# Forgetting attention with stationary values for two heads side by side, its weights scaled by VectorE, and the recurrence's head norm on VectorE

## The reference

```python
def rms_norm_f32(x, g):
    return xf * lax.rsqrt(jnp.mean(xf * xf, axis=-1, keepdims=True) + EPS) * g

# hgrn2, behind the scan over chunks; o: (B, S, 4 heads, 128)
    o = rms_norm_f32(o, norm_g)
    gate = jax.nn.silu(g).reshape(B, S, HGRN_HEADS, HGRN_DIM)
    return (o * gate).reshape(B, S, HALF)

def forgetting_attention(q, k, v, f_logit, b_f):
    c = jnp.cumsum(jax.nn.log_sigmoid(f_logit + b_f), axis=1).transpose(0, 2, 1)
    for blk in range(S // Q_BLOCK):                       # 4 query tiles of 128
        q0, q1 = blk * Q_BLOCK, (blk + 1) * Q_BLOCK
        logits = jnp.einsum('bqhd,bkhd->bhqk', q[:, q0:q1], k[:, :q1]) * scale
        logits = logits + c[:, :, q0:q1, None] - c[:, :, None, :q1]
        logits = jnp.where(kpos <= qpos, logits, -jnp.inf)
        p = jax.nn.softmax(logits, axis=-1)
        outs.append(jnp.einsum('bhqk,bkhd->bqhd', p, v[:, :q1]))

# the layer
    ya = hgrn2(...); yb = forgetting_attention(...)
    mix = jnp.concatenate([ya, yb], axis=-1) @ ev_w_out[e]
```

## Time and profile before

| | us |
|---|---|
| median of 3 runs | 2923.24 (2921.44 to 2928.81) |
| the profiled execution | 2928.32 |
| its span, first to last instruction | 2926.4 |
| PE busy | 2849.7 (97%) |
| DVE busy | 1678.2 (57%) |
| ACT busy | 1073.3 (37%) |
| POOL busy | 993.9 (34%) |
| first scores of the forgetting attention | at 1889.0 |
| first output product behind it | at 1941.70 |

### The profile page before, as it was taken

The page is one execution under the profiler, slowest core; times in us unless marked ns, Lnnn a source line. Parts: engine busy times, 40 slices in busy tenths (PEclk is TensorE's granted clock), DMA queues, the critical chain, the costliest instruction groups (busy, mean ns, idle before and its releaser), DMA issues.

```text
span 2926.4 us, 42935 instructions
## 1 busy us (share of the span) xinstructions
PE 2849.7 (97%) x17688; PEld 2509.3 (86%) x17688; DVE 1678.2 (57%) x2092; ACT 1073.3 (37%) x1792; POOL 993.9 (34%) x795
## 2 busy tenths in 40 slices
PE   8989999999999999999999999999999998999998
PEld 7877888999888768889998887789998886699987
DVE  3844513988335495048882334738884247598832
ACT  2235313544124373235441221545442233454411
POOL 5840261000647612610016467530006464000063
PEclk9998999999999999999999999999999998999999
DMA  4341341433223203314322332004332232043322
GB/s 143 102 137 37 102 143 44 140 99 95 91 97 109 86 16 113 132 44 137 102 80 101 98 102 96 16 15 138 113 97 87 87 108 72 23 140 106 95 87 87
DMA packets 185862, 271.69 MB, mean 93 GB/s; under 512 B 7988, under 2 KB 147252, under 8 KB 185668
## 3 DMA queue, kind: packets, MB, share of 16 engines
q1 hardware_dynamic: 175520, 243.29, 25.6%
q10 hardware_dynamic: 10148, 25.66, 2.6%
HBM read 266.79 MB, written 2.13 MB: 92 GB/s over the span
## 4 chain that ended last, share of the span: by engine, by line
PE 81%; DVE 11%; issue 3%; DMA 2%; ACT 2%; POOL 1%; ACTq 0%; SPq 0%; DVEq 0%; POOLq 0%
PE PS L498 24%; PE PS L500 24%; PE PS L499 24%; PE PS L949 3%; PE PS L589 2%; DVE a_qk L1666 2%; PE PS L911 1%; POOL wlo L2781 1%; DVE nmx L2001 1%; PE PS L1105 1%; DVE s_c L2651 1%; PE PS L1852 1%; DVE rawb_r L1264 1%; DVE d_a L1995 0%; DMA rawb<-ffn_w 0%
## 5 line engine op out<-in xcount | busy, mean ns | idle before, releaser
L2781 POOL TENSOR_TENSOR wlo<-raw,whi 128x512 fp32r<-128x512 f32 x502 | 680.7, 1386 | 602.8 <-ACT whi L668 602.8
L2773 POOL TENSOR_SCALAR whi<-raw 128x1024 fp32r<-128x1024 f32 x224 | 258.9, 1175 | 1189.6 <-PE PS L500 814.3
L498 PE MATMUL PS<-xT_hi,ring_r 128*128 128x256 f32 x1280 | 362.5, 283 | 1.3 <-issue 1.3
L499 PE MATMUL PS<-xT_lo,ring_r 128*128 128x256 f32 x1280 | 362.2, 283 | 0.0
L498 PE MATMUL PS<-xT_hi,whi 128*128 128x512 f32 (+1 forms) x1024 | 349.0, 341 | 10.9 <-DVE xT_lo L609 6.4
L499 PE MATMUL PS<-xT_lo,whi 128*128 128x512 f32 (+1 forms) x1024 | 345.2, 337 | 0.0
L500 PE MATMUL PS<-xT_hi,wlo 128*128 128x512 f32 (+1 forms) x1024 | 345.1, 337 | 0.0
L498 PE MATMUL PS<-sum_hi_r,ring_r 128*128 128x256 f32 x960 | 272.5, 284 | 5.1 <-DVE u_u L1362 5.1
L498 PE MATMUL PS<-whi,hs_hi 128*128 128x512 f32 x704 | 274.7, 390 | 1.0 <-issue 1.0
L500 PE MATMUL PS<-whi,hs_lo 128*128 128x512 f32 x704 | 274.0, 389 | 0.0
L499 PE MATMUL PS<-wlo,hs_hi 128*128 128x512 f32 x704 | 274.0, 389 | 0.0
(11 more groups left out here) (438 smaller groups left out, 6026.7 us busy)
## 6 DMA issues: line engine op xcount, KB each, us to landing
rawb<-ffn_w_gu SPq DMA_DIRECT2D x60, 512.0 KB, 3.6
rawb<-ffn_w SPq DMA_DIRECT2D x60, 512.0 KB, 3.6
raw<-ffn_w SPq DMA_DIRECT2D x26, 1024.0 KB, 4.9
raw<-ffn_w_down SPq DMA_DIRECT2D x22, 1024.0 KB, 4.9
raw<-mem_wkv SPq DMA_DIRECT2D x16, 1024.0 KB, 5.4
raw<-even_w_in SPq DMA_DIRECT2D x14, 1024.0 KB, 5.1
raw<-ev_w_in SPq DMA_DIRECT2D x14, 1024.0 KB, 5.2
raw<-odd_w_in SPq DMA_DIRECT2D x12, 1024.0 KB, 5.1
```

The source lines that it names most:

```text
L498: pe.matmul(o, lhs[0], rhs[0], start=start, stop=False, skip_group_check=True)
L499: pe.matmul(o, lhs[0], rhs[1], start=False, stop=False, skip_group_check=True)
L2773: pool.tensor_scalar(whi[b][:, cs], raw[b][:, cs], 1.0, 1.0, ALU.mult, ALU.mult).then_inc(panel_hi, 1)
L2781: m = pool.tensor_tensor(wlo[b][:, cs], raw[b][:, cs], whi[b][:, cs].bitcast(F32), ALU.subtract)
```

## The change

- The forgetting attention becomes `direct`: values stand still (64 columns, one head in each half of the columns), transposed weights of 128 columns stream, the output comes transposed and goes from PSUM into `xT_hi` and `xT_lo` (`act_direct`, `dve_direct`). `store` no longer scales, and `g_row`'s last 512 columns are not used.
- The softmax weights are scaled instead: `scale(u)` on DVE makes one reciprocal for two units and scales their `f_p` in place, behind the statistics of the odd units, two units back. PE's transposes wait for the new semaphore `f_scaled`.
- `f_p` has 6 buffers, `lag` is 4, `behind` is 7. The buffers move into the area of dead tiles, and `f_c1` moves so that it is not overwritten.
- The head norm's three products for each tile go from POOL to DVE (`norm(t)`), behind units 13, 15, 17 and 19. The power stays on POOL.
- At the end PE transposes only the recurrence's half of each tile (4 blocks).

```diff
@@ -257,10 +258,10 @@
         g_khr = w("g_khr", [P, S])
         g_qh = w("g_qh", [P, S])
         g_state = w("g_state", [P, NT, P])
-        f_c1 = w("f_c1", [P, 4, S])
-        w = Area("X")
+        w = Area("W")
+        f_p = w("f_p", [P, 6, 512])
         f_add = w("f_add", [P, 2, 512])
-        f_p = w("f_p", [P, 3, 512])
+        w = Area("W", 4 * (4 + 4 + 4) * S)
         f_pt = w("f_pt", [P, 2, 512])
 
         w = Area("W")
...
@@ -989,9 +988,9 @@
         def softmax_exp(act, A, u, src, scale, width, p):
 
             act.wait_ge(stat_ready, A.u0 + u + 1)
-            if u >= 3:
-
-                act.wait_ge(pt_psum, A.u0 + u - 2)
+            if u >= A.ps_:
+
+                act.wait_ge(pt_psum, A.u0 + u - A.ps_ + 1)
             act.activation(p[:, 0:width], src, ACT.Exp, bias=nmx[:, u:u + 1], scale=scale,
                            accum_out=rsum[:, u:u + 1]).then_inc(exp_done, 1)
...
@@ -2066,11 +2065,12 @@
 
         def stage_hgrn(st, jobs):
             A = Units(8 * NT, lambda u: u // 8 + 1, [0, 1, 2, 3], [4, 5], [6, 7], lambda u: u // 8, stat_ready,
-                      lambda u: f_p[:, u % 3, :], lambda u: f_pt[:, u % 2, :], lambda u: u % 8 == 7)
-            A.together = 2
+                      lambda u: f_p[:, u % 6, :], lambda u: f_pt[:, u % 2, :], lambda u: u % 8 == 7, direct=True)
+            A.together, A.lag, A.ps_, A.behind = 2, 4, 6, 7
             names = ["f_cut", "f_sum", "f_read", "f_abs", "f_ln", "f_bc", "f_bc_read",
                      "lb_in", "lb_exp", "lb_done", "g_lf", "g_scan", "g_din", "g_exp", "g_ops", "g_sc", "g_msk", "g_cpy",
-                     "g_inter", "g_kht", "g_khc", "g_kv", "g_st", "g_store", "gq_in", "gq_done", "gs_in", "g_rms", "g_norm"]
+                     "g_inter", "g_kht", "g_khc", "g_kv", "g_st", "g_store", "gq_in", "gq_done", "gs_in", "g_rms", "g_norm",
+                     "f_scaled"]
             G = {n: S_(n) for n in names}
             chunk = lambda c: slice(128 * c, 128 * c + 128)
             NL = 8
...
@@ -2230,9 +2230,13 @@
 
                     if 1 <= u <= NT:
                         act.activation(g_b[:, u - 1, :], g_row[:, u - 1, 0:512], ACT.Square).then_inc(G["gq_done"], 1)
+                    if u % 8 == 1 and u > 8:
+                        act_direct(act, 4, A.ob(u - 2), A.group(u - 2), A.u0 + u - 1)
                 act_units(act, A, lambda u: softmax_exp(act, A, u, f_add[:, u % 2, 0:128 * A.nk(u)], -1.0,
                                                         128 * A.nk(u), A.p(u)), squares)
-                act_rows(act, 0, KD)
+                act_direct(act, 4, A.ob(A.n - 1), NT - 1, A.u0 + A.n)
+                for t in range(NT):
+                    act_turn(act, xT_hi, 0, 4, 2 * t, t)
 
             def dve(dve, step):
                 dve.wait_ge(*loads["levels"])
...
@@ -2376,9 +2380,31 @@
                         dve.wait_ge(G["gq_done"], t + 1)
                         step(dve.tensor_reduce(scol[:, 16 + 4 * t:20 + 4 * t],
                                                g_b[:, t, :].rearrange("p (h d) -> p h d", h=4), AX_X, ALU.add))
+                    if u in (13, 15, 17, 19):
+                        norm((u - 13) // 2)
                     if u == 6 + NT:
                         dve.tensor_scalar(scol[:, 16:32], scol[:, 16:32], 1.0 / 128, EPS, ALU.mult, ALU.add)\
                             .then_inc(G["gs_in"], 1)
+
+                def scale(u):
+
+                    dve.wait_ge(exp_done, A.u0 + u + 2)
+                    step(dve.reciprocal(rec[:, u:u + 2], rsum[:, u:u + 2]))
+                    for v in (u, u + 1):
+                        p = A.p(v)[:, 0:128 * A.nk(v)]
+                        dve.tensor_scalar(p, p, rec[:, v:v + 1], None, ALU.mult).then_inc(G["f_scaled"], 1)
+
+                def norm(t):
+
+                    if t == 0:
+                        dve.wait_ge(G["g_rms"], 1)
+                    v = g_row[:, t, 0:512].rearrange("p (h d) -> p h d", h=4)
+                    for n, factor in enumerate((scol[:, 4 * t:4 * t + 4].unsqueeze(2).to_broadcast([P, 4, 128]),
+                                                pcol("norm_g").unsqueeze(1).to_broadcast([P, 4, 128]),
+                                                g_g[:, t, :].rearrange("p (h d) -> p h d", h=4))):
+                        if n:
+                            dve.wait_ge(G["g_norm"], 3 * t + n)
+                        dve.tensor_tensor(v, v, factor, ALU.mult).then_inc(G["g_norm"], 1)
 
                 def stat(u):
                     t, h = u // 8, u % 8
...
@@ -2390,15 +2416,17 @@
                     dve.tensor_tensor_reduce(out=f_add[:, u % 2, 0:n], in0=PS[:, A.ps(u), 0:n], in1=f_c(h)[:, 0:n],
                                              scale=-1.0, scalar=-NEG, op0=ALU.add, op1=ALU.min,
                                              accum_out=nmx[:, u:u + 1]).then_inc(stat_ready, 1)
+                    if u % 2 == 1 and u >= 3:
+                        scale(u - 3)
+                    if u == A.n - 1:
+                        scale(u - 1)
                     norms(u)
 
                 def store(g, bank):
-                    step(dve.reciprocal(rec[:, 8 * g:8 * g + 8], rsum[:, 8 * g:8 * g + 8]))
-                    return dve.tensor_tensor(g_row[:, g, 512:1024].rearrange("p (h d) -> p h d", h=8),
-                                             PS[:, bank, :].rearrange("p (h d) -> p h d", h=8),
-                                             rec[:, 8 * g:8 * g + 8].unsqueeze(2).to_broadcast([P, 8, 64]), ALU.mult)
+                    dve_direct(dve, 4, bank, g)
                 dve_units(dve, A, stat, store)
-                dve_rows(dve, 0, KD)
+                for t in range(NT):
+                    dve_turn(dve, xT_hi, xT_lo, 0, 4, 2 * t, t)
 
             def pool(pool):
...
@@ -2411,16 +2439,6 @@
 
                 pool.wait_ge(G["gs_in"], 1)
                 pool.tensor_tensor(scol[:, 0:16], scol[:, 16:32], rec[:, 32:48], ALU.pow).then_inc(G["g_rms"], 1)
-                pool.wait_ge(G["g_rms"], 1)
-                n = 0
-                for t in range(NT):
-                    v = g_row[:, t, 0:512].rearrange("p (h d) -> p h d", h=4)
-                    for factor in (scol[:, 4 * t:4 * t + 4].unsqueeze(2).to_broadcast([P, 4, 128]),
-                                   pcol("norm_g").unsqueeze(1).to_broadcast([P, 4, 128]),
-                                   g_g[:, t, :].rearrange("p (h d) -> p h d", h=4)):
-                        pool.tensor_tensor(v, v, factor, ALU.mult).then_inc(G["g_norm"], 1)
-                        n += 1
-                        pool.wait_ge(G["g_norm"], n)
 
             def pe(pe):
                 pe_split(pe, jobs, 1)
...
@@ -2513,10 +2531,16 @@
 
                 def values(u, k):
                     h = u % 8
-                    return f_v[:, k, 64 * h:64 * h + 64], 64 * h, 64
-                pe_units(pe, A, scores, values, lambda u: (exp_done, A.u0 + u + 1))
+                    return f_v[:, k, 64 * h:64 * h + 64], slice(64 * (h % 2), 64 * (h % 2) + 64), 128 * (h // 2)
+                pe_units(pe, A, scores, values, lambda u: (G["f_scaled"], u + 1))
+                n_turn["pe"] += NT
                 pe.wait_ge(G["g_norm"], 3 * NT)
-                pe_rows(pe, g_row, KD, lambda t: A.g0 + t + 1)
+                before = n_turn["pe"]
+                for t in range(NT):
+                    if t == 3:
+
+                        pe.wait_ge(lo_ready, before - 1)
+                    pe_turn(pe, g_row[:, t, 0:512], 4, 2 * t)
             return {"act_load": act_load, "act": act, "dve": dve, "pe": pe, "pool": pool}
 
         def stage_lru(st, jobs):```

The norm on DVE comes to stand between the scaling of units 10 and 11 and the statistics of unit 14. DVE's list before, from behind the statistics of unit 10 to those of unit 12 (`f_add` and `nmx` are the statistics of one unit); from there to unit 18 it holds statistics alone:

```order
L2380 TENSOR_SCALAR scol<-scol 128x16
L2390 ISA f_add,nmx<-PS,f_c_211 128x256
L2390 ISA nmx 128x1
L2396 RECIPROCAL rec<-rsum 128x8
L2397 TENSOR_TENSOR g_row<-PS,rec 128x512
L2390 ISA f_add,nmx<-PS,f_c_224 128x256
L2390 ISA nmx 128x1
```

7 lines of the change are left out of this document (3 added, 4 removed).

## The result

The changed kernel took 2929.16 us (median of 18 runs, 2924.67 to 2943.06), the kernel before 2924.72 us in the same session (18 runs, 2919.76 to 2933.42). The ratio is 1.0021, 95% interval 1.0012 to 1.0030: slower by 0.2% (the two medians alone are 1.0015 apart, which the interval holds). The forecast was 2929.0 us and +0.20%. The profiled execution has a span of 2926.6 us. The total is right; the terms that make it up are partly wrong and partly cancel, as the traces show, so that the closeness of the sum is luck.

What follows compares the result with a forecast made beforehand. PE sets the pace, busy 97% of the span. Terms -4.4 - 1.5 + 1.0 + 1.1 + 5.6 + 4.0 = +5.8 us gave 2929.0 us by the median (+0.20%), range 2918.5 to 2936.

Steps and rivals of the forecast that it cites:

- value products: Forgetting attention on PE: pairs of units get shorter, as in the lru stage's form; -4.4 us.
- tail: Attention's end: sixteen output-row transposes fewer, but the first output product waits for a chain; 3.6 to 2.1, -1.5 us.
- drain: Attention's last pairs: PE idles for copies held up by the two transposed-weight buffers; +1.0 us.
- squares, units 6 to 9: DVE also sums squares there, so PE waits for the scaling of units 6 and 8; +1.1 us.
- norm's place and collision: DVE's norm ahead of statistics and scaling makes PE wait, +5.6 us; POOL's split lengthens DVE's instructions, +4.0 us.
- over 5 us: Unit 12 of the attention: PE's wait for weights would grow from 1.6 to over 5 us.
- its last part: List of signs: PE waits for scaled weights at units 12, 14, 16 and 18, the first over 4 us.
- The clock falls: Rival: PE's idle time in the attention drops its clock for some 20 us; +5 us more, 2934.0 us; chance 0.27.
- No collision: Rival: POOL's split meets mostly statistics or its panel is held up; +1.8, 2925.0 us; chance 0.17.
- The norm hides too: Rival: PE's head start and six weight buffers cover DVE's norm; -3.8, 2919.4 us; chance 0.15.
- The heads do not overlap: Rival: two heads' value products run one behind the other, 4.4 us not gained; +10.2, 2933.4 us; chance 0.04.
- price for DVE's scalings: Attention on DVE: a plain pair costs 1.5 to 2.3 us against PE's 2.5 to 3.7, so hidden.

Runs made afterwards that it cites:

- e10: e6, but POOL's panel split is held until DVE has scaled the last pair of weights; 2918.47 us, ratio 0.9988 to the kernel before.
- e2: The changed kernel, but POOL waits for the end of DVE's head norm before it splits its panel; 2927.25 us, ratio 1.0020 to the kernel before.
- e11: The changed kernel with only POOL's panel split held until the last scaling; 2926.10 us, ratio 1.0021 to the kernel before.
- e3: The changed kernel with four buffers for the transposed weights instead of two; 2927.48 us, ratio 1.0019 to the kernel before.
- e6: The changed kernel with POOL's split ahead of the attention, four transposed buffers, norm products spread singly over units 14 to 30; 2924.23 us, ratio 1.0003.
- e4: The kernel before with only the head norm moved from POOL to DVE, old value products kept; 2928.81 us, ratio 1.0020.
- e7: e6 with the two heads' value products one behind the other instead of alternating; 2926.28 us, ratio 1.0019 to the kernel before.
- e9: e6, but POOL's panel split waits until DVE has laid its last mask of the recurrence; 2918.77 us, ratio 0.9986 to the kernel before.
- e1: The changed kernel with the head norm's twelve products back on POOL; 2924.44 us, ratio 1.0008 to the kernel before.
- e8: The changed kernel with the norm back on POOL, POOL's split ahead of the attention, four transposed buffers; 2927.89 us, ratio 1.0011.
- e5: The changed kernel with POOL's panel split moved ahead of the attention, before the wait for the norm's input; 2930.79 us, ratio 1.0023.

## Why the prediction was right, and where it was not

The direction and the mechanism held: PE waits for DVE, which norms and scales beside POOL's split. The sum held by luck: +5.8 us forecast; +6.4 by the path, +6.1 by the ratio. Term by term, with what the traces show for the changed kernel:

| term | forecast | measured | from |
|---|---|---|---|
| value products | -4.4 | -3.45 | PE's time up to the last value product, idle out: 48.77 before, 45.32 in e10 |
| tail | -1.5 | -1.45 | 3.70 to 2.25 |
| drain | +1.0 | +1.74 | 0.38 + 0.34 + 0.24 + 0.78 at the end |
| squares, units 6 to 9 | +1.1 | 0 | no wait for a scaling there |
| norm's place and collision | +5.6, +4.0 | +4.7 | waits 3.66 + 0.50 + 0.54 |
| short waits for a buffer | none | about +2.5 | an estimate, below |
| low clock | rival | about +2.2 | 4.89 against 2.66 |

The measured column sums to about +6.3. The stage grew by 6.75, and the kernel before had 0.23 us of idle time of its own, so 0.7 us have no term. The norm, the collision and the squares were forecast 6.0 us too high; what the forecast lacked or had too low adds up to 6.5 us.

**Right.** The value products of two heads side by side and the tail, by rows of another stage with the same form. From four-block scores to the sixteen value records PE takes 2.14 us (1928.31 to 1930.45), in the lru stage 2.13 (2510.55 to 2512.68), and the records take 1.09 in both. (1924.56 to 1928.31 is 3.75 us, close to the 3.74 of the four-block pair in the forecast, but it is another thing: it holds only twelve value records and one short stop. Without the stop it is 3.53 us in e10.) The step "splits the waiting weight panel at once: ... exactly while DVE norms tile 0 and scales" is what the trace shows, and the prices of the earlier trace rows (1.45, 1.60) are those of the collision here (1.41 to 1.64). e2 and e11 take the split away from the norm with nothing else changed, and the long wait and the low clock go both times.

**Wrong: the size of the norm's term.** It rests on DVE's turn being longer than PE's. DVE's was within the forecast of 3.7 to 4.3 us: in e11 the waits for scalings are 3.74, 3.80 and 3.86 us apart. But "PE has in that time ... 2.5 us with two blocks, 3.1 with three" was too small. With the 0.62, 0.69 and 0.54 us of these waits taken off, PE's own turn is 3.1 us, and 3.3 with three blocks. The records alone take 2.66 us in e10; the rest are the short stops, which the forecast lacked, and what a stop costs beside its idle time. So the four norms cost 2.3 us of waiting (e11) instead of 5.6. In the changed kernel the norm and the collision together are 4.7 us of waiting, not 9.6. No wait reached the "over 5 us" of the forecast, nor the four that its last part asked for, and there were three waits and not four: behind the long one, at the low clock, PE did not wait at unit 14.

**Wrong: the squares.** The forecast took 1.1 us for them. In the changed kernel PE waits for no scaling at units 6 to 9; where the short stops are gone, one wait of 0.20 us appears there (e3, e6, e10).

**Missed: the two transposed buffers.** The forecast charged them at the end of the stage only. Its prices came from rows of the lru stage, and that stage has four (`A.pts, A.turn_first = 4, True`), so that the rows could not show the stop. Eleven short waits of 0.16 us are 1.7 us by the list of waits. A stop costs more than its idle time, since the records on both sides no longer overlap: with four-block scores and three-block products, pairs are 3.54 us apart in e11 and 3.31 in e10 without the stop, 0.23 each, over eleven pairs about 2.5 us. That is an estimate of what they cost by themselves; taken away alone (e3) they give back 1.4, since PE then waits longer for the norm.

**Right number, wrong reason: the end of the stage.** The last wait was forecast as 0.7 us and is 0.78, but the forecast laid it on the two buffers. With four buffers it is still 0.78 (e3, e6 and e10): the last product needs the copy of the last unit, that copy begins when this unit's transposes are done, and PE has nothing left to do beside it. In e10:

```profile
1929.33 1.09 PE L940 MATMUL PS<-f_pt,f_v 128*64 128x128 f32 x16 [0.78 <-ACT f_pt L961]
```

**The rivals.** *The clock falls* was partly true: it fell where PE stood still, but came back after 6 us (10 in e4), not 20, so the price was about 2 us and not 5. Whether it falls is not settled by the wait alone, as e6 and e7 show, so the 2 us are those of the profiled execution and not surely of the median. *No collision* fell with the first norm product. *The norm hides too* is false at the places that the change chose, and true in e9 and e10, where the products go one by one and POOL's split is out of the way. *The heads do not overlap* is false: e7 puts one head behind the other and loses 2.5 us by it. The forecast's price for DVE's scalings had them hidden except beside the norm and the squares; e1 and e8 show that they collide with POOL as well where the norm stays on POOL. They are hidden only while POOL is not on SBUF.

**What stays open.** How much of e11's gain over the change reaches the total; why the value products gain 3.45 us and not 4.4, since no run changes them alone; how much of the changed kernel's loss the low clock is in the median run; and why a low-clock stretch follows some waits of PE and not others, and lasts 3 to 10 us.

## What to carry to other kernels

Before you move SBUF work to an engine that is half idle, ask what its neighbour on SBUF does at that moment *once the work is gone from it*: the engine that was relieved runs ahead to its next job, and here that job landed on the very instructions that PE waits for. Then look for a place where both can't meet; moving POOL's split by a single wait was worth 4.4 us of the path (e6 to e9) with no work removed, some 1.3 of them by the clock. And measure a local length in the trace as well as one a stage earlier: e6 looked like a gain of 2.8 us in its stage and was none.

## What the runs showed of the hardware

- DVE and POOL on SBUF at once: DVE's pair of scalings of 256 columns goes from 0.62 to 2.38 (changed kernel) and 2.76 us (e1), one of 384 columns from 0.75 to 2.82 (e1), and a norm product from 0.69 to between 1.41 and 1.64. POOL's own products beside them kept 1.04 to 1.28 us (e1); its split went from 7.0 to between 7.4 (e1: 2.06 + 5.29) and 9.2 us (e4: 2.49 + 6.72). DVE pays more.
- The 1.2 GHz level followed PE's waits unevenly. A wait of 3.10 us in the recurrence was followed by some 6 us of it in e5, some 3 in e6 and e8, and none in e7. 3.66 (changed kernel) and 4.25 us (e3) were followed by 6 to 7 us, 1.53 us (e4) by 10, and 1.41 us (e2) by none, nor were sums of idle of 6 to 7 us in the stage in short pieces (e5, e11).
- Sixteen value records (64 stationary columns each, 128 streamed) take 1.09 us with the two column halves alternating and 1.58 one half after the other. The Trainium skill, page "TensorEngine Tiling (Array Packing)", section "Theoretical Speedup", has up to 2x for such tiles; here the alternation gives 1.45. Against the old form's 1.96 us, where the weights stand and the values stream, it is 1.8.
- Twelve waits of 0.16 us look like 1.9 us in the list of waits, but a pair with one is 0.23 us longer than a pair without (e11 against e10).
